# A chunked scan: masks straight from the chunk matrices' banks, two corner products with full weights

## The chip, the cores and the metric

The program runs on one core of a Trainium2 chip. The metric is the device time of one execution in microseconds; where several runs were made, their median stands. One further execution was recorded by the hardware profiler, and all rows below come from it.

## What is computed

The reference is a model of three blocks on a sequence of 1024 tokens with 1024 features, in float32: a first block with two mixers side by side (an RWKV-7 scan and an mLSTM) and a convolved feed-forward part, then two layers of gated attention. The change touches only the RWKV-7 scan, 8 heads of 64 channels:

```
def rwkv7_scan(r, w, k, v, a, b):
    def step(S, inp):
        r_t, w_t, k_t, v_t, a_t, b_t = inp
        sa = jnp.einsum('bhij,bhj->bhi', S, a_t)
        S = S * w_t[:, :, None, :] + sa[..., None] * b_t[:, :, None, :] + v_t[..., :, None] * k_t[..., None, :]
        y = jnp.einsum('bhij,bhj->bhi', S, r_t)
        return S, y
```

## The kernel before

The program is written engine by engine, each with its own list of instructions and semaphores between them. Nothing is scheduled by a tool: the order of each list is the order written.

The scan works on chunks of 64 tokens, two chunks (e = 0, 1) at a time, eight pairs in all, each for 8 heads (h, with j = h // 2 and q = h % 2). With the decays folded into `AR` (rates and receptances, features on partitions) and `BK` (keys and gains), a chunk's recurrence becomes products of 64 x 64 matrices and the inverse of one unit triangular matrix per head and chunk. For one pair the TensorE list is:

1. `chunk_matrices`: for each head and chunk the product gains x rates (L753, into banks 6 and 7) and its transpose (L759, banks 4 and 5); then `products(e)` (L768, banks 2e and 2e + 1), which gives for each head the whole 128 x 128 matrix of keys and gains against rates and receptances; then transposes of values (L775), keys (L781) and rates (L784).
2. `inverse`: it starts from the diagonal blocks (`i_X`) and joins blocks of growing size in five levels. Level n is `corner(n)` (L800: the part `i_O[n]` off the diagonal, times `i_X`), then a VectorE addition of the identity (`i_T`, L2450), then `joined(n)` (L825 and L827), whose results ScalarE (L1730, L1734) and VectorE (L2445) copy back to `i_X` and `i_XT`. After level 0's corner `flip` (L812) makes `i_XT`. Level 4 ends in `last` (L841). Each step is done in two halves of four heads, so that the copies of one half lie beside the products of the other.
3. Between these steps stand the pieces of the previous pair's `chain`: value products (L882), two halves of the solve (L899), transitions (L910), inputs (L921), the state and carried products (L931, L944) and local ones (L951). They use the solved inverse of the pair before.

VectorE masks the first product to `i_LT` (L2429), the second to `i_X` (L2433), adds the identity (L2435) and copies the values (L2437, L2438). GpSimd then makes the five `i_O[n]` from `i_LT` (L481), one operation each, and masks both copied matrices `GB` (L487). ScalarE copies `products(e)` to `GB` (L1714), the transposed keys behind them (L1719), which also frees bank 4 for the value products, and the rates (L1722). In level 1 it copies the solution (L1699, L1700) after VectorE's `W` (L2393), ahead of `i_X` for corner 2. The masks themselves (`level_masks`) are made once on GpSimd; `i_X` of the first pair waits for the last of them.

Of the kernel before, what the change touches and what calls it, by code (L numbers as in the profile page):

```python
# [20 lines left out]
ALU = mybir.AluOpType  # L21
ACT = mybir.ActivationFunctionType

P = 128
# [82 lines left out]
def build(nc, xin, vec, w_lora, consts, cmask, rope, lnm, band, ws, park, out):  # L107
    with ExitStack() as ctx:
# [105 lines left out]
        LEVELS, MASK_STEPS = 5, 18  # L214
# [29 lines left out]
        i_O = [at(f"off{n}", YH + (4 + n) * 2 * K, [P, 8, CH]) for n in range(LEVELS)]  # L244
        i_Z = at("inv_z", YH + 18 * K, [P, 8, CH])
# [165 lines left out]
        def _(pool):  # L411
# [37 lines left out]
            def level_masks():  # L449
# [21 lines left out]
                pool.wait_ge(sem("rp_done"), 4)  # L471
                merge(MSK_LOW, 7, 1)
# [4 lines left out]
            def chunk_pair(i):  # L477

                pool.wait_ge(sem("c_LT"), 2 * i + 1)
                for n in range(LEVELS):  # L480
                    pool.tensor_tensor(i_O[n][:, :, :], i_LT[:, :, :],  # L481
                                       msk[:, MSK_LEVEL[n], :].unsqueeze(1).to_broadcast([P, 8, CH]), ALU.mult
                                       ).then_inc(sem("c_off"), 1)
# [27 lines left out]
        def _(pe):  # L511
# [229 lines left out]
            def chunk_matrices(i):  # L741
# [8 lines left out]
                for h in range(8):  # L750
                    j, q = h // 2, h % 2
                    for e in range(2):
                        mm = pe.matmul(bank(6 + q)[rows(e), j * CH:(j + 1) * CH], gains(j, q, i, e), rates(j, q, c + e),  # L753
                                       start=True, stop=True)
                mm.then_inc(sem("c_Q"), 1)
                for h in range(8):
                    j, q = h // 2, h % 2
                    for e in range(2):
                        mm = pe.matmul(bank(4 + q)[rows(e), j * CH:(j + 1) * CH], rates(j, q, c + e), gains(j, q, i, e),  # L759
# [13 lines left out]
                pe.wait_ge(sem("c_LT"), 2 * i + 1)  # L773
# [4 lines left out]
                pe.wait_ge(sem("c_LT"), 2 * i + 2)  # L778
# [8 lines left out]
            def inverse(i, pieces):  # L787

                def corner(n, beside=None):  # L790
                    for half in range(2):
# [6 lines left out]
                        for h in range(4 * half, 4 * half + 4):  # L798
                            for e in range(2):
                                mm = pe.matmul(bank(inv_set(n, half))[own_rows(e), h % 4 * CH:(h % 4 + 1) * CH],  # L800
                                               i_O[n][rows(e), h, :], i_X[rows(e), h, :], start=True, stop=True)
# [4 lines left out]
                def flip():  # L806

                    pe.wait_ge(sem("c_Gcopied"), 2 * i + 2)
                    for half in range(2):
                        for h in range(4 * half, 4 * half + 4):  # L810
                            for e in range(2):
                                mm = pe.matmul(bank(inv_set(1, half))[own_rows(e), h % 4 * CH:(h % 4 + 1) * CH],  # L812
                                               i_X[rows(e), h, :], ident[rows(e), rows(e)], start=True, stop=True)
# [2357 lines left out]
```

## Time and profile before

| | us |
|---|---|
| median of 3 runs | 3541.15 (3540.38 to 3541.54) |
| the profiled execution | 3542.03 |
| its span from the first to the last instruction | 3540.2 |

```profile
PE 89%; DVE 6%; ACT 2%; issue 1%; POOL 1%; DMA 1%; ACTq 0%; DVEq 0%; POOLq 0%; SPq 0%
```

This line of the page is the chain of work that ended last, followed back from the last instruction, in shares of the span by engine. PE is TensorE's matmuls, PEld its weight loads, which overlap them, DVE is VectorE, ACT ScalarE, POOL GpSimd and SP SyncE. Matmuls are pipelined, so the length of one is more than its share of TensorE's time: what a row of them costs is read from their starts, or from the length of the whole row less the last one's own length. In the rows below x32 is the number of instructions, and what stands in brackets behind a row is the idle time ahead of it and what ended it.

### The profile page before, as it was taken

How to read it: one execution, taken by the hardware profiler on the slowest of the kernel's cores; microseconds unless marked ns; L12 is line 12 of the kernel's file. 1: busy time of each engine (PE TensorE's matmuls, PEld its weight loads, DVE VectorE, ACT ScalarE, POOL GpSimd, SP SyncE). 2: the span in 40 equal slices, each digit the busy share in tenths (PEclk: the TensorE clock that was granted, in tenths of full speed). 3: DMA queues.
4: the chain of work that ended last, by engine and by line, in shares of the span. 5: the costliest groups of instructions: out<-in, count | busy, mean ns of one | idle time of the engine just before them, and what ended most of it. 6: DMA issues, size and time to landing. Idle time of an engine off the chain costs nothing.

```text
span 3540.2 us, 55064 instructions
## 1 busy us (share of the span) xinstructions
PE 3374.2 (95%) x22562; PEld 2700.3 (76%) x22562; DVE 1872.9 (53%) x2515; ACT 781.1 (22%) x1269; POOL 1203.2 (34%) x571
## 2 busy tenths in 40 slices
PE   7999598999999999989999999999989999999997
PEld 6878488788888888867777678888867677688886
DVE  7444655546676676664545554433546554434434
ACT  4211443211101101133323320000323332300001
POOL 3324044233444443332222224434322222244444
PEclk9999699999999999999999999999999999999998
DMA  4111000221111111131112121111321111211111
GB/s 138 42 64 41 1 4 4 75 72 48 47 47 47 47 47 52 43 115 54 43 48 54 37 84 48 47 49 52 109 65 43 48 42 48 78 48 48 47 48 66
DMA packets 55226, 189.56 MB, mean 54 GB/s; under 512 B 6448, under 2 KB 15376, under 8 KB 53408
## 3 DMA queue, kind: packets, MB, share of 16 engines
q1 hardware_dynamic: 38016, 135.85, 12.1%
q10 hardware_dynamic: 17056, 51.44, 4.6%
q8 instruction: 123, 2.02, 0.2%
q14 instruction: 31, 0.25, 0.0%
HBM read 165.07 MB, written 14.86 MB: 51 GB/s over the span
## 4 chain that ended last, share of the span: by engine, by line
PE 89%; DVE 6%; ACT 2%; issue 1%; POOL 1%; DMA 1%; ACTq 0%; DVEq 0%; POOLq 0%; SPq 0%
PE ps L527 55%; PE ps L1041 10%; PE ps L1425 5%; PE ps L1213 3%; PE ps L1240 3%; PE ps L1258 3%; DVE sc L2787 1%; PE ps L800 1%; PE ps L1167 1%; PE ps L1069 1%; PE ps L825 1%; PE ps L768 1%; PE ps L899 0%; DVE hL L2287 0%; DMA cMo<-out 0%
## 5 line engine op out<-in xcount | busy, mean ns | idle before, releaser
L417 POOL TENSOR_TENSOR wH<-wraw,pv 128x1024 fp32r<-128x1024 f32 x239 | 465.1, 1946 | 2105.6 <-PE ps L527 1711.5
L527 PE MATMUL ps<-hH,wH 128*128 128x512 f32 x2800 | 880.3, 396 | 30.9 <-DVE hL L2287 11.8
L527 PE MATMUL ps<-hL,wH 128*128 128x512 f32 x2800 | 872.5, 393 | 0.0
L527 PE MATMUL ps<-hH,wL 128*128 128x512 f32 x2800 | 870.5, 392 | 0.0
L527 PEld LDWEIGHTS ps<-hH,wH 128*128 128x128 f32 x2800 | 522.0, 189 | 142.5 <-issue 20.6
L419 POOL TENSOR_TENSOR wL<-wraw,wH 128x1024 fp32r<-128x1024 f32 x239 | 623.2, 2607 | 18.8
L527 PEld LDWEIGHTS ps<-hL,wH 128*128 128x128 f32 x2800 | 525.9, 189 | 110.5 <-issue 1.7
L527 PEld LDWEIGHTS ps<-hH,wL 128*128 128x128 f32 x2800 | 525.5, 189 | 108.6
L2569 DVE TENSOR_TENSOR xT<-ps,xT 128x512 f32<-128x512 f32 x544 | 361.5, 689 | 6.6 <-PE ps L1069 6.6
L2890 DVE TENSOR_TENSOR sg<-ps,mrows 128x1024 f32<-128x1024 f32 x46 | 56.3, 1225 | 372.0 <-PE ps L527 372.0
L1928 ACT ACTIVATE sc<-sc,stat 128x256 f32<-128x256 f32 (+7 forms) x256 | 170.9, 668 | 126.9 <-DVE stat L2794 66.4
L1213 PE MATMUL ps<-kP,qP 64*128 64x256 f32 (+3 forms) x672 | 139.4, 514 | 44.3 <-DVE stat L2794 40.9
L2030 ACT ACTIVATE sg<-sg 128x1024 f32<-128x1024 f32 x46 | 48.8, 1061 | 557.9 <-DVE sg L2890 557.9
L1240 PEld LDWEIGHTS ps<-cst,sc 128*128 128x128 f32 x900 | 99.6, 144 | 77.1 <-issue 64.6
L1240 PE MATMUL ps<-cst,sc 128*128 128x128 f32 x900 | 152.7, 291 | 4.2 <-ACT sc L1928 4.1
L1213 PEld LDWEIGHTS ps<-kP,qP 64*128 64x128 f32 x672 | 56.4, 192 | 103.8 <-DVE stat L2794 47.8
L1258 PE MATMUL ps<-pt,vtok 128*64 128x128 f32 x1800 | 128.1, 282 | 0.0
L1041 PE MATMUL ps<-gH,wH 128*128 128x512 f32 x320 | 125.8, 393 | 0.0
L1041 PE MATMUL ps<-gL,wH 128*128 128x512 f32 x320 | 124.7, 390 | 0.0
L1041 PE MATMUL ps<-gH,wL 128*128 128x512 f32 x320 | 124.7, 390 | 0.0
L1258 PEld LDWEIGHTS ps<-pt,vtok 128*64 128x64 f32 x1800 | 97.4, 138 | 24.8 <-issue 23.9
L2787 DVE CUSTOM_DVE_ANT_0 sc<-ps,lnM 128x128 f32<-128x128 f32 (+7 forms) x96 | 72.7, 757 | 71.4 <-PE ps L1213 66.7
(434 smaller groups left out, 4301.7 us busy)
## 6 DMA issues: line engine op xcount, KB each, us to landing
wraw<-ws SPq DMA_DIRECT2D x242, 512.0 KB, 3.6
park<-xT ACTq DMA_DIRECT2D x2, 4096.0 KB, 13.2
xT<-park ACTq DMA_DIRECT2D x2, 4096.0 KB, 12.3
recT<-out ACTq DMA_DIRECT2D x28, 256.0 KB, 3.9
xT<-xin SPq DMA_DIRECT2D x4, 1024.0 KB, 9.1
xT<-xin ACTq DMA_DIRECT2D x1, 4096.0 KB, 12.4
sc<-kraw ACTq DMA_DIRECT2D x32, 128.0 KB, 2.4
out<-xT SPq DMA_DIRECT2D x16, 256.0 KB, 2.1
```

Source lines behind the costliest of these rows:

```text
L417: pool.tensor_tensor(wH[:, j, :], wraw[:, j, :], zero, ALU.add).then_inc(w_hi, 1)
L419: pool.tensor_tensor(wL[:, j, :], wraw[:, j, :], wH[:, j, :], ALU.subtract).then_inc(w_ready[j], 1)
L527: mm = pe.matmul(pair(p)[:, half * HALF:(half + 1) * HALF], wp, hp[:, k, half * HALF:(half + 1) * HALF], start=(m == 0 and n == 0), stop=( ...
L1041: mm = pe.matmul(pair(2 + e % 2)[:, half * HALF:(half + 1) * HALF], w[:, j, e * P:(e + 1) * P], h[:, half * HALF:(half + 1) * HALF], start ...
L1213: mm = pe.matmul(outs[j][:, c:e], qP[r, n * P:(n + 1) * P], kP[r, k0 + c - c0:k0 + e - c0], start=True, stop=True)
L1240: mm = pe.transpose(out[:, c:c + P], (SC[0] if br == "C" else SC[n % 2])[:, j, b + c:b + c + P], ident)
L1258: mm = pe.matmul(out[r, :], vtok[:, v + 64 * j:v + 64 * j + 64], pt[:, j, b + c:b + c + P], start=(c == c0), stop=(c + P == c1))
L1425: mm = pe.matmul(pair(p)[:, half * HALF:(half + 1) * HALF], wp, hp[:, k, half * HALF:(half + 1) * HALF], start=(k == k0 and n == 0), stop= ...
L1928: act.activation(buf[:, j, b + c0:b + c1], buf[:, j, b + c0:b + c1], ACT.Exp, bias=stat[:, S_NEG, s:s + 1], accum_out=stat[:, S_DEN, s:s + ...
L2569: ins = dve.tensor_tensor(x, bank(2 * pairs[e % len(pairs)] + half), x, ALU.add)
L2787: dve.tensor_tensor_reduce(buf[:, j, b + c0:b + c1], bank(0, 4)[:, o + c0:o + c1], bias, 1.0, -3e38, op, ALU.max, mx).then_inc(sem("at_ttr ...
L2890: dve.tensor_tensor(gates[g], pair(j), mrows[:, :], ALU.mult).then_inc(sem("sg_raw"), 1)
```

## The change

In each pair the product gains x rates (L753) is dropped. The same block is a quarter of what `products(e)` computes, on the partitions 64 to 127 for chunk 0 and 0 to 63 for chunk 1, and VectorE masks it from there into `i_LT`, one operation for each chunk on 64 partitions. So `i_LT` and all that follows from it in the inverse lie on the opposite halves from before, and the slices of partitions change places in `corner`, `flip`, `joined` and `last`. `c_LT` now counts three steps per pair (i_X, then i_LT of chunk 0 and of chunk 1); GpSimd starts after the third, and ScalarE's copy of each matrix waits until VectorE has read it. The corners 1 and 2 get weights of 128 x 128 per head (`i_F`), in which the two chunks' blocks stand off the diagonal and the rest is zero, through two masks of twice the width (`f_msk`), which GpSimd makes in eight more steps; each is then one product per head over the whole array, where there were two in quarters.

```
--- before.py
+++ after.py
@@ -211,7 +211,7 @@
         MSK_LOW, MSK_EYE = 0, 7
-        LEVELS, MASK_STEPS = 5, 18
+        LEVELS, MASK_STEPS = 5, 26
         INV_ACT, INV_DVE, INV_PROD = 12, 18, 30
         MSK_LEVEL = (2, 3, 6, 5, 4)
         eye = msk[:, MSK_EYE, :]
@@ -242,6 +242,9 @@
         AT = [at(f"AT{n}", YH + (5 + n) * TILE, [P, 8, 2 * CH]) for n in range(2)]
         i_LT, i_X, i_XT, i_T = [at(f"inv{n}", YH + n * 2 * K, [P, 8, CH]) for n in range(4)]
         i_O = [at(f"off{n}", YH + (4 + n) * 2 * K, [P, 8, CH]) for n in range(LEVELS)]
+        FULL = (1, 2)
+        i_F = {n: at(f"full{n}", o, [P, 8, 2 * CH]) for n, o in zip(FULL, (YH + 10 * K, YH + 28 * K))}
+        f_msk = at("full_msk", XA + 28 * K, [P, len(FULL), 2, CH])
         i_Z = at("inv_z", YH + 18 * K, [P, 8, CH])
         W = at("W", WR + 4 * TILE, [P, 8, CH])
         MT = at("MT", YL + TILE, [P, 2, 4, CH])
@@ -469,6 +472,11 @@
                 step(pool.tensor_tensor(m(3), m(3), m(2), ALU.subtract))
                 step(pool.tensor_tensor(m(2), m(2), m(1), ALU.subtract))
                 pool.wait_ge(sem("rp_done"), 4)
+                for k, n in enumerate(FULL):
+                    for e in range(2):
+                        home, away = (slice(64, 128), slice(0, 64)) if e == 0 else (slice(0, 64), slice(64, 128))
+                        step(pool.memset(f_msk[away, k, e, :], 0.0))
+                        step(pool.tensor_copy(f_msk[home, k, e, :], msk[home, MSK_LEVEL[n], :]))
                 merge(MSK_LOW, 7, 1)
                 step(pool.tensor_tensor(m(MSK_LOW), m(MSK_LOW), m(7), ALU.subtract))
                 step(pool.tensor_tensor(m(MSK_LOW), m(MSK_LOW), m(1), ALU.subtract))
@@ -476,8 +484,15 @@
             def chunk_pair(i):
-                pool.wait_ge(sem("c_LT"), 2 * i + 1)
+                pool.wait_ge(sem("c_LT"), 3 * i + 3)
                 for n in range(LEVELS):
+                    if n in FULL:
+                        shape = [P, 8, 2, CH]
+                        pool.tensor_tensor(i_F[n][:, :, :].rearrange("p h (e t) -> p h e t", e=2),
+                                           i_LT[:, :, :].unsqueeze(2).to_broadcast(shape),
+                                           f_msk[:, FULL.index(n), :, :].unsqueeze(1).to_broadcast(shape), ALU.mult
+                                           ).then_inc(sem("c_off"), 1)
+                        continue
                     pool.tensor_tensor(i_O[n][:, :, :], i_LT[:, :, :],
                                        msk[:, MSK_LEVEL[n], :].unsqueeze(1).to_broadcast([P, 8, CH]), ALU.mult
                                        ).then_inc(sem("c_off"), 1)
@@ -750,13 +765,7 @@
                 for h in range(8):
                     j, q = h // 2, h % 2
                     for e in range(2):
-                        mm = pe.matmul(bank(6 + q)[rows(e), j * CH:(j + 1) * CH], gains(j, q, i, e), rates(j, q, c + e),
-                                       start=True, stop=True)
-                mm.then_inc(sem("c_Q"), 1)
-                for h in range(8):
-                    j, q = h // 2, h % 2
-                    for e in range(2):
-                        mm = pe.matmul(bank(4 + q)[rows(e), j * CH:(j + 1) * CH], rates(j, q, c + e), gains(j, q, i, e),
+                        mm = pe.matmul(bank(4 + q)[own_rows(e), j * CH:(j + 1) * CH], rates(j, q, c + e), gains(j, q, i, e),
                                        start=True, stop=True)
                 mm.then_inc(sem("c_Q"), 1)
@@ -770,12 +779,11 @@
                     mm.then_inc(sem("c_G"), 1)
                 products(0)
-                pe.wait_ge(sem("c_LT"), 2 * i + 1)
                 for j in range(4):
                     mm = pe.transpose(bank(7)[:, j * P:(j + 1) * P], vpad[:, j, (c + 1) * CH:(c + 3) * CH], ident)
                 mm.then_inc(sem("c_tokT"), 1)
                 products(1)
-                pe.wait_ge(sem("c_LT"), 2 * i + 2)
+                pe.wait_ge(sem("c_LT"), 3 * i + 1)
                 for e in range(2):
                     for j in range(4):
                         mm = pe.transpose(bank(4 + e)[:, j * P:(j + 1) * P], BK[:, j, i, e * P:(e + 1) * P], ident)
@@ -796,9 +804,14 @@
                         else:
                             pe.wait_ge(sem("inv_act"), i * INV_ACT + 3 * n - 2 + half)
                         for h in range(4 * half, 4 * half + 4):
+                            at_h = slice(h % 4 * CH, (h % 4 + 1) * CH)
+                            if n in FULL:
+                                mm = pe.matmul(bank(inv_set(n, half))[:, at_h], i_F[n][:, h, :], i_X[:, h, :],
+                                               start=True, stop=True)
+                                continue
                             for e in range(2):
-                                mm = pe.matmul(bank(inv_set(n, half))[own_rows(e), h % 4 * CH:(h % 4 + 1) * CH],
-                                               i_O[n][rows(e), h, :], i_X[rows(e), h, :], start=True, stop=True)
+                                mm = pe.matmul(bank(inv_set(n, half))[rows(e), at_h], i_O[n][own_rows(e), h, :],
+                                               i_X[own_rows(e), h, :], start=True, stop=True)
                                 if beside:
                                     beside(h, e)
                         mm.then_inc(sem("inv_prod"), 1)
@@ -809,8 +822,8 @@
                     for half in range(2):
                         for h in range(4 * half, 4 * half + 4):
                             for e in range(2):
-                                mm = pe.matmul(bank(inv_set(1, half))[own_rows(e), h % 4 * CH:(h % 4 + 1) * CH],
-                                               i_X[rows(e), h, :], ident[rows(e), rows(e)], start=True, stop=True)
+                                mm = pe.matmul(bank(inv_set(1, half))[rows(e), h % 4 * CH:(h % 4 + 1) * CH],
+                                               i_X[own_rows(e), h, :], ident[own_rows(e), own_rows(e)], start=True, stop=True)
                         mm.then_inc(sem("inv_prod"), 1)
                 def joined(n):
@@ -822,10 +835,10 @@
                         for h in range(4 * half, 4 * half + 4):
                             for e in range(2):
                                 at_h = slice(h % 4 * CH, (h % 4 + 1) * CH)
-                                x = pe.matmul(bank(inv_set(n + 1, half))[rows(e), at_h], i_XT[own_rows(e), h, :],
-                                              i_T[own_rows(e), h, :], start=True, stop=True)
-                                xt = pe.matmul(bank(inv_set(n, half))[own_rows(e), at_h], i_T[own_rows(e), h, :],
-                                               i_XT[own_rows(e), h, :], start=True, stop=True)
+                                x = pe.matmul(bank(inv_set(n + 1, half))[own_rows(e), at_h], i_XT[rows(e), h, :],
+                                              i_T[rows(e), h, :], start=True, stop=True)
+                                xt = pe.matmul(bank(inv_set(n, half))[rows(e), at_h], i_T[rows(e), h, :],
+                                               i_XT[rows(e), h, :], start=True, stop=True)
                         x.then_inc(sem("inv_prod"), 1)
                         xt.then_inc(sem("inv_prod"), 1)
@@ -839,7 +852,7 @@
                         for h in range(4 * half, 4 * half + 4):
                             for e in range(2):
                                 mm = pe.matmul(bank(inv_set(n + 1, half))[rows(e), h % 4 * CH:(h % 4 + 1) * CH],
-                                               i_T[own_rows(e), h, :], i_XT[own_rows(e), h, :], start=True, stop=True)
+                                               i_T[rows(e), h, :], i_XT[rows(e), h, :], start=True, stop=True)
                         mm.then_inc(sem("inv_prod"), 1)
                 corner(0, pieces and pieces["values"])
@@ -1711,6 +1724,7 @@
                 p = i % 2
                 for e in range(2):
                     act.wait_ge(sem("c_G"), i * 2 + e + 1)
+                    act.wait_ge(sem("c_LT"), 3 * i + e + 2)
                     act.activation(GB[p][:, e, :, 0:2 * CH].rearrange("p (j q) x -> p q j x", q=2),
                                    bank(2 * e, 2).rearrange("p (q j x) -> p q j x", q=2, x=P), ACT.Copy
                                    ).then_inc(sem("c_Gcopied"), 1)
@@ -2425,13 +2439,17 @@
                 def mask4(n):
                     return n.unsqueeze(1).unsqueeze(1).to_broadcast([P, 2, 4, CH])
-                dve.wait_ge(sem("c_Q"), 2 * i + 1)
-                dve.tensor_tensor(by_parity(i_LT), stacked(6), mask4(cst[:, C_G, 0:CH]), ALU.mult).then_inc(sem("c_LT"), 1)
-                dve.wait_ge(sem("c_Q"), 2 * i + 2)
+                dve.wait_ge(sem("c_Q"), i + 1)
                 if i == 0:
                     dve.wait_ge(sem("pool_own"), MASK_STEPS + 1)
                 dve.tensor_tensor(by_parity(i_X), stacked(4), mask4(msk[:, MSK_LOW, :]), ALU.mult).then_inc(sem("c_LT"), 1)
-                dve.wait_ge(sem("c_LT"), 2 * i + 2)
+                for e in range(2):
+                    home = slice(64, 128) if e == 0 else slice(0, 64)
+                    dve.wait_ge(sem("c_G"), 2 * i + e + 1)
+                    block = ps[home, 2 * e:2 * e + 2, :].rearrange("p q (j x) -> p q j x", x=P)[:, :, :, 0:CH]
+                    upper = cst[home, C_G, 0:CH].unsqueeze(1).unsqueeze(1).to_broadcast([64, 2, 4, CH])
+                    dve.tensor_tensor(by_parity(i_LT)[home], block, upper, ALU.mult).then_inc(sem("c_LT"), 1)
+                dve.wait_ge(sem("c_LT"), 3 * i + 1)
                 dve.tensor_tensor(i_X[:, :, :], i_X[:, :, :], mask(eye, 8), ALU.add).then_inc(sem("c_X"), 1)
                 dve.wait_ge(sem("c_tokT"), 4 * i + 1)
                 dve.tensor_copy(UV[i % 2][0:64, 0, :, :], bank(7)[0:64, :])
```

## Rows read from the trace of the kernel before

**Rows 1.** The page: busy time of each engine, its share of the span.

```profile
PE 3374.2 (95%) x22562; PEld 2700.3 (76%) x22562; DVE 1872.9 (53%) x2515; ACT 781.1 (22%) x1269; POOL 1203.2 (34%) x571
```

**Rows 2.** Windows, a chunk pair and the scan: PE, PEld, DVE, ACT, POOL, clock, DMA.

```profile
510.80:536.80 26.00, 23.56 (x821) 21.29 (x819) 13.67 (x29) 9.82 (x21) 11.29 (x7) 1.00 0.02 4
...
438.50:642.30 203.80, 184.04 (x6273) 166.45 (x6274) 107.06 (x217) 76.55 (x164) 91.16 (x59) 0.99 0.02 4
```

**Rows 3.** Waits of TensorE in the scan: total us, times, longest.

```profile
PE ps L827 <- issue: 3.5, 4, 1.2
...
PE ps L800 <- ACT inv L1730: 1.9, 4, 0.5
...
PE ps L910 <- issue: 0.2, 1, 0.2
```

**Rows 4.** Windows from idle time to idle time, weight loads alone (PEld busy, count).

```profile
584.98:588.62 3.64, 2.44 (x126) 1.00 0.02 5
588.62:592.60 3.98, 3.53 (x127) 1.00 0.03 6
```

**Rows 5.** DMA queues in the scan's stretch.

```profile
q8 instruction: 49, 0.80, 1.7%
```

**Rows 6.** Timeline of the start of a pair: start us, length us, what, count.

```profile
512.10 0.64 PE L759 MATMUL ps<-BK,AR 64*64 64x64 f32 x30
512.33 0.69 DVE L2429 TENSOR_TENSOR inv<-ps,cst 128x512 f32<-128x512 f32 x1 [0.82 <-PE ps L753]
...
513.65 1.27 DVE L2435 TENSOR_TENSOR inv<-inv,msk 128x512 f32<-128x512 f32 x1
...
514.85 0.67 DVE L2437 COPY UV<-ps 64x512 f32<-64x512 f32 x1
515.44 1.09 PE L781 MATMUL ps<-cst,BK 128*128 128x128 f32 x8
...
515.56 1.02 ACT L1714 ACTIVATE GB<-ps 128x1024 f32<-128x1024 f32 x1 [0.65 <-PE ps L768]
516.37 0.60 PE L784 MATMUL ps<-cst,AR 128*128 128x128 f32 x4
516.48 1.08 ACT L1719 ACTIVATE GB<-ps 128x512 f32<-128x512 f32 x2
516.90 0.32 PE L800 MATMUL ps<-inv,off 64*64 64x64 f32 x2
517.12 0.27 PE L882 MATMUL ps<-UV,GB 64*64 64x64 f32 x1
```

**Rows 7.** Timeline of GpSimd: the last masks, and one pair.

```profile
438.58 0.29 POOL L458 TENSOR_TENSOR msk<-msk 128x64 f32<-128x64 f32 x1 [85.44 <-DVE BK L2385]
...
439.35 0.32 POOL L474 TENSOR_TENSOR msk<-msk 128x64 f32<-128x64 f32 x1
...
513.10 6.66 POOL L481 TENSOR_TENSOR off<-inv,msk 128x512 f32<-128x512 f32 x5 [15.62 <-DVE inv L2429]
519.69 4.69 POOL L487 TENSOR_TENSOR GB<-GB,cst 128x1024 f32<-128x1024 f32 x2
```

**Rows 8.** Timelines from corner 1 to corner 2: TensorE, VectorE and ScalarE.

```profile
521.80 1.13 PE L800 MATMUL ps<-inv,off 64*64 64x64 f32 x32
522.50 0.89 DVE L2450 TENSOR_TENSOR inv<-ps,msk 128x256 f32<-128x256 f32 x2 [1.31 <-PE ps L800]
523.31 0.68 DVE L2393 COPY W<-ps 128x512 f32<-128x512 f32 x1
...
524.62 0.59 ACT L1700 ACTIVATE UV<-ps 64x512 f32<-64x512 f32 x1
525.12 0.64 ACT L1730 ACTIVATE inv<-ps 128x256 f32<-128x256 f32 x2
...
525.63 1.15 PE L800 MATMUL ps<-inv,off 64*64 64x64 f32 x32
```

**Rows 9.** Timeline of TensorE: full weights with one moving column.

```profile
1543.64 1.93 PE L540 MATMUL ps<-cst,nsum_g 128*128 128x1 f32 x16
```

More of the change, by code:

```diff
@@ L244, in build @@
         i_O = [at(f"off{n}", YH + (4 + n) * 2 * K, [P, 8, CH]) for n in range(LEVELS)]
+        FULL = (1, 2)
+        i_F = {n: at(f"full{n}", o, [P, 8, 2 * CH]) for n, o in zip(FULL, (YH + 10 * K, YH + 28 * K))}
+        f_msk = at("full_msk", XA + 28 * K, [P, len(FULL), 2, CH])
         i_Z = at("inv_z", YH + 18 * K, [P, 8, CH])
@@ L471, in level_masks @@
                 pool.wait_ge(sem("rp_done"), 4)
+                for k, n in enumerate(FULL):
+                    for e in range(2):
+                        home, away = (slice(64, 128), slice(0, 64)) if e == 0 else (slice(0, 64), slice(64, 128))
+                        step(pool.memset(f_msk[away, k, e, :], 0.0))
+                        step(pool.tensor_copy(f_msk[home, k, e, :], msk[home, MSK_LEVEL[n], :]))
                 merge(MSK_LOW, 7, 1)
@@ L477, in chunk_pair @@
             def chunk_pair(i):
[L479 removed]
+                pool.wait_ge(sem("c_LT"), 3 * i + 3)
                 for n in range(LEVELS):
+                    if n in FULL:
+                        shape = [P, 8, 2, CH]
+                        pool.tensor_tensor(i_F[n][:, :, :].rearrange("p h (e t) -> p h e t", e=2),
+                                           i_LT[:, :, :].unsqueeze(2).to_broadcast(shape),
+                                           f_msk[:, FULL.index(n), :, :].unsqueeze(1).to_broadcast(shape), ALU.mult
+                                           ).then_inc(sem("c_off"), 1)
+                        continue
                     pool.tensor_tensor(i_O[n][:, :, :], i_LT[:, :, :],
@@ L752, in chunk_matrices @@
                     for e in range(2):
[L753 to L759, printed above, removed]
+                        mm = pe.matmul(bank(4 + q)[own_rows(e), j * CH:(j + 1) * CH], rates(j, q, c + e), gains(j, q, i, e),
                                        start=True, stop=True)
@@ L798, in corner @@
                         for h in range(4 * half, 4 * half + 4):
+                            at_h = slice(h % 4 * CH, (h % 4 + 1) * CH)
+                            if n in FULL:
+                                mm = pe.matmul(bank(inv_set(n, half))[:, at_h], i_F[n][:, h, :], i_X[:, h, :],
+                                               start=True, stop=True)
+                                continue
                             for e in range(2):
-                                mm = pe.matmul(bank(inv_set(n, half))[own_rows(e), h % 4 * CH:(h % 4 + 1) * CH],
-                                               i_O[n][rows(e), h, :], i_X[rows(e), h, :], start=True, stop=True)
+                                mm = pe.matmul(bank(inv_set(n, half))[rows(e), at_h], i_O[n][own_rows(e), h, :],
+                                               i_X[own_rows(e), h, :], start=True, stop=True)
                                 if beside:
@@ L811, in flip @@
                             for e in range(2):
-                                mm = pe.matmul(bank(inv_set(1, half))[own_rows(e), h % 4 * CH:(h % 4 + 1) * CH],
-                                               i_X[rows(e), h, :], ident[rows(e), rows(e)], start=True, stop=True)
+                                mm = pe.matmul(bank(inv_set(1, half))[rows(e), h % 4 * CH:(h % 4 + 1) * CH],
+                                               i_X[own_rows(e), h, :], ident[own_rows(e), own_rows(e)], start=True, stop=True)
                         mm.then_inc(sem("inv_prod"), 1)
```

28 lines of the change are left out of this document (16 added, 12 removed).

## The prediction

> **What bounds the kernel now.** I began with the page's line of busy times [rows 1]: TensorE is busy for 95% of the span. The profiled execution took 3542.03 us against a median of 3541.15, so a change of the profile's length can be added to the median as it stands. A stretch that grows on TensorE's queue moves the end by as much, if nothing there was waiting. The change touches only the scan, which the stretches by chunk pair place between 438.5 and 642.3 us, with a period of some 26 us [rows 2]. There TensorE's busy column reads 184.0 of 203.8 us, but that doesn't say that the array is at its peak, so the second question was what ends its idle times. The list of waits has ten rows "issue" for TensorE in the scan, 3.5 us the longest and 0.2 the shortest; their sum is 16.6 us in 26 idle times, and the only other steady row is 1.9 us behind ScalarE's copy [rows 3]. "Issue" means that nothing in the profile was waited for. What it is can be read by laying windows from the end of one such idle time to the end of the next: each holds 126 or 127 weight loads and as many matmuls, some 253 instructions with the waits between them left out, and takes 3.64 or 3.98 us [rows 4]. The scan's weight loads and matmuls together (6273 and 6274) divided by 256 are 49, and the queue for instructions moved 49 packets of 16 KB in it [rows 2, 5]. So TensorE's instructions arrive in blocks of 256, a block can't be entered before about 3.75 us have gone since the last one was entered, and dense stretches of small products run ahead of that. The scan has two limits that alternate: this delivery of instructions, and the chain product, VectorE or ScalarE copy, next product.
>
> The Trainium skill, Runtime: NRT & Kernel Launch, section "Instruction fetch mechanics", gives the same 16 KB and 256 instructions, but says that the fetch is hidden behind the issue of the instructions. The 26 idle times speak against that here; if it held, the give-back below would be nothing and the time 3561.6.
>
> **The change part by part**, per chunk pair, of which there are eight.
>
> *Removed: the 16 products of L753.* Each is two passes (32 records per pair). Their twin L759 uses all four quarters of the array too: 30 passes in 0.64 us, of which 0.22 is the last one's own length, so 15 ns a pass [rows 6]. 32 x 15 ns is **0.49 us** less, all on TensorE's queue.
>
> *The start of the inversion.* Before, VectorE masks i_LT (0.69 us) and i_X as well, and adds the identity (1.27) while TensorE still makes the chunk matrices [rows 6]. Afterwards i_LT comes out of the banks of these matrices, in two halves of 64 partitions. A copy of 64 x 512 takes 0.67 us where one of 128 x 512 takes 0.69 [rows 6], so halving the partitions saves nothing: two operations of 0.68, the second only after the last matrix. Behind that second one wait: ScalarE's copy of the second matrix (it now waits for c_LT too; 1.02 us) with the copies of the keys queued behind it (a pair in 1.08 us), which free bank 4 for the value products; GpSimd's first off-diagonal mask (five in 6.66 us, 1.3 each [rows 7]); and, queued on VectorE itself, the addition of the identity. Today the copy starts at 515.56 and the first value product at 517.12, 1.56 later [rows 6]. Now 0.69 goes in front of it: 2.25 after the last matrix. The mask gives 0.69 + 1.3 and two handovers of some 0.05, 2.1; the identity 0.69 + 1.27 and one handover, 2.0. All three arrive together, so the cost is 0.7 to 0.8; I take **0.75**. The values' copies (c_X) then end near 518.5 in these times, and VectorE's first eye addition slips by about a microsecond, but the first solve product (16 passes in about 0.9 us) lies between it and the joined product, so this stays covered. If that cover were gone it would cost up to 0.5.
>
> *Two corners with full weights.* Corner 1 is 32 passes of 64 by 64 from 521.80, 1.13 us with the last one's 0.22: 28 ns a pass, or 57 per pair of quarters [rows 8]. Now it is 8 products, 16 passes, with 128 x 128 weights and 64 columns moving. No row of before has this form. The nearest are the 16 passes with 128 x 128 weights and a single moving column: 1.93 us less 0.25 over 15 intervals, 112 ns [rows 9]; and the transposes with 128 columns moving: 8 in 1.09 less 0.28 over 7, 116 [rows 6]. One column or 128 cost the same, so here it is the loading of 128 weight columns that counts, and 64 moving columns lie between the two. The other end is 57 ns, if a full load went as fast as the two quarters that it replaces. I take 112, since both neighbours stand on either side of the new shape: 16 x 0.112 = 1.79 against 0.91, **0.88** more per corner, 1.76 for the two. Is it on the path? After corner 1 VectorE makes T (0.89 for both halves), then copies W (0.68), ScalarE copies UV twice (0.59 each) and i_X (0.64 for two), and only then corner 2 starts [rows 8]. The whole corner is in front of that chain. Behind corner 2 TensorE's own queue goes on with products that wait for nothing late. So both count in full.
>
> *Going between tile sizes.* From the last 128 x 128 transpose to the first 64 x 64 product TensorE takes longer than within either: the four transposes begin at 516.37 and step by some 0.11, so the last begins at 516.70, and the product comes at 516.90, 0.20 later [rows 6]. In minus the steady step I take 0.10 for leaving full size and 0.15 for entering it (there also the second pass comes late), so **0.50** per pair; the ends are 0, where a wait covers it, and 0.7. The Trainium skill, TensorEngine Tiling (Array Packing), section "Tiling Modes", says that a change of mode drains the engine, which speaks against putting two full corners amid quarters. The trace agrees, by the 0.20. Without such a cost the time forecast would be 3550.6.
>
> *Masks and GpSimd.* The masks FULL for corners 1 and 2 have 1024 elements per partition rather than 512; the nearest row is 4.69 for two, 2.35 each, against 1.3 [rows 7]: GpSimd works 2.1 us more per pair and starts 3 us later. Corner 1's mask is then ready at about 519.9 and starts to be wanted at 521.80, corner 2's at 522.3 against 525.6; the masked GB at 530 is wanted by the next pair after 540. Nothing. Once only, eight more small steps stand before X's mask: three take from 438.58 to 439.67 [rows 7], so 3 us more, mostly under the first pair's matrices: 0.3 in all.
>
> *Instructions.* L753's 32 passes and the 16 saved in each full corner are 64 passes, 128 instructions with their loads, of some 1640 per pair; 1024 over the scan, four blocks. If every block were waited for, this returned 4 x 3.75 = 15 us. Of 49 blocks 26 are, so I take half, **7 us** in total; the ends are 0 and 15.
>
> **Sum:** 8 x (-0.49 + 0.75 + 1.76 + 0.50) + 0.3 = 20.5; less 7 is +13.5. On the profiled execution 3555.5, on the median **3554.6**.
>
> **The rivals.**
> *A, the other side: delivery of instructions is the real bound.* If a block costs 3.75 us whatever is in it, the added array time falls into idle time that is there anyway, and 128 instructions fewer give 1.9 us per pair, 15 in all: 3526. For it: a block's mean time in the scan is 203.8/49 = 4.16 us, close to 3.75. Against: the idle time for it is 16.6 us in all, and lies in the second half of each pair, while corners 1 and 2 and the start lie in the first, where blocks take five and more. It decides from where the added 20.5 us falls by more than two thirds into those idle times. With cheap full loads (57 ns) the same mechanism gives 20.5 - 14 - 4 - 7, 3536.6. Chance 0.13.
> *B, about even:* half of the added time is covered by blocks that were late anyway, and the return is 12: 8 x 2.5 x 0.7 - 12 = +2, 3543. Chance 0.15.
> *C, nothing comes back:* blocks stay as late as they are, since the dense second half hardly changes; +20.5 and dearer changes of tile size 1.6: 3563. For it: in that half only L753 goes. Chance 0.12, within the slower cases.
> That the change doesn't do what it says isn't a rival: the products and their quarters are plain in the diff.
>
> **How the numbers follow.** The forecast and C together have 0.72, A 0.13, B 0.15. About 0.2% (7 us) is what a measurement of this kernel can tell from no change: slower by more 0.72, within it 0.15, faster 0.13. The range leaves out A and reaches over most of B and up to C: 3541 to 3563.
>
> **What would show it.** In the profile after: L753's pass over the gains gone; L800 in two forms, the full one with 256 records, 16 to a corner in about 2.0 us from first to last end (right: 105 to 120 ns a pass; 60 or 80 would take the forecast away); the value products 2.2 to 2.4 us behind the last matrix; the scan some 13.5 us longer; four packets of instructions fewer and the "issue" rows near 10 us rather than 16.6. If these rows fall to nearly nothing, A or B was right; if they stay at 16, C.

## The result and the profile after

The changed kernel takes 3549.23 us at the median of 13 runs, the one before 3541.15. The ratio is 1.0024, with a 95% interval of 1.0015 to 1.0033: slower by 8.5 us, between 5.3 and 11.7. So it lies between 3546.5 and 3552.9. The forecast was 3554.6 within 3541 to 3563: the range holds the measured time, but the forecast itself lies above the interval.

The profiled executions differ by a little more, 3553.22 against 3542.03 us; the first is the second slowest of its 13 runs. All scans below are from one execution each. First the stretch of the scan in both, from its first product to the first product behind it (columns: length, then busy time and count for PE, PEld, DVE, ACT and POOL, the granted clock, the share of the DMA engines, GB/s). Before:

```profile
438.50:654.00 215.50, 193.37 (x6528) 174.84 (x6528) 111.17 (x225) 78.92 (x168) 91.16 (x59) 0.99 0.02 4
```

After:

```profile
438.90:665.60 226.70, 201.64 (x6017) 182.66 (x6017) 111.52 (x233) 78.92 (x168) 109.32 (x67) 0.99 0.02 4
```

The scan is 11.2 us longer; the rest of the span is the same within half a microsecond. TensorE is busy for 8.3 us more with 511 matmuls fewer, and idle for 25.1 instead of 22.1. What it is idle for (waits of TensorE in the scan: total us, times, longest) has changed:

```profile
PE ps L813 <- POOL off L496: 8.4, 8, 1.1
PE ps L809 <- ACT inv L1744: 3.4, 7, 0.5
PE ps L944 <- issue: 2.9, 4, 1.1
PE ps L813 <- issue: 1.7, 2, 0.9
PE ps L957 <- issue: 1.6, 2, 0.9
PE ps L840 <- issue: 1.5, 3, 0.7
PE ps L964 <- issue: 1.3, 2, 0.7
PE ps L838 <- issue: 0.8, 2, 0.6
```

The "issue" rows, which answer to those of [rows 3], sum to 9.8 us in 15 idle times, where it was 16.6 in 25 (the prediction counts 26, but the ten rows sum to 25). A new wait stands above them: in each of the eight pairs corner 0 (now L813) waits for GpSimd's first mask. It can be followed in the timeline of one pair, which answers to [rows 6]:

```profile
519.55 1.09 PE L789 MATMUL ps<-cst,BK 128*128 128x128 f32 x8
519.67 0.68 DVE L2451 TENSOR_TENSOR inv<-ps,cst 64x512 f32<-64x512 f32 x1 [0.99 <-PE ps L777]
520.28 0.67 DVE L2453 TENSOR_TENSOR inv<-inv,msk 128x512 f32<-128x512 f32 x1
520.43 1.65 POOL L496 TENSOR_TENSOR off<-inv,msk 128x512 f32<-128x512 f32 x1 [14.05 <-DVE inv L2451]
520.45 1.02 ACT L1728 ACTIVATE GB<-ps 128x1024 f32<-128x1024 f32 x1 [0.64 <-DVE inv L2451]
520.48 0.60 PE L792 MATMUL ps<-cst,AR 128*128 128x128 f32 x4
...
521.37 1.08 ACT L1733 ACTIVATE GB<-ps 128x512 f32<-128x512 f32 x2
...
522.13 0.27 PE L813 MATMUL ps<-inv,off 64*64 64x64 f32 x1 [1.05 <-POOL off L496]
522.24 0.24 PE L895 MATMUL ps<-UV,GB 64*64 64x64 f32 x1
```

The second chunk matrix is there at 519.67, and the first value product (L895) comes at 522.24, 2.57 us later, where it was 1.56 (515.56 to 517.12 in [rows 6]). GpSimd's mask takes 1.65 us, and TensorE begins right behind it. The full corners in the same pair, which answer to [rows 8]:

```profile
527.03 2.00 PE L809 MATMUL ps<-inv,full 128*128 128x64 f32 x16
530.15 1.10 PE L923 MATMUL ps<-GB,W 64*64 64x128 f32 x32
531.73 1.97 PE L809 MATMUL ps<-inv,full 128*128 128x64 f32 x16 [0.48 <-ACT inv L1744]
533.63 0.69 PE L934 MATMUL ps<-UV,GB 128*64 128x64 f32 x16
```

Sixteen passes take 2.00 us. Less the last one's 0.27 over 15 intervals that is 115 ns a pass: 160 ns for the first interval and 111 or 112 for all others. From the last of them to the first product in quarters it takes 0.2 us. In the DMA view the queue for instructions moved 48 packets where the same stretch of before had 52.

### The profile page after: what moved, and what is told of

It reads as the page before. It is cut to its first block, busy times and chain, and to the rows that moved or that the text cites. A ratio compares the mean times of both kernels' runs of the same rounds, so it can differ in the third digit from the quotient of the medians.

```text
span 3550.9 us, 54071 instructions
## 1 busy us (share of the span) xinstructions
PE 3381.5 (95%) x22050; PEld 2706.4 (76%) x22050; DVE 1874.0 (53%) x2523; ACT 781.6 (22%) x1269; POOL 1222.6 (34%) x579
## 4 chain that ended last, share of the span: by engine, by line
PE 89%; DVE 6%; ACT 2%; issue 1%; POOL 1%; DMA 1%; ACTq 0%; DVEq 0%; POOLq 0%; SPq 0%
PE ps L542 55%; PE ps L1054 10%; PE ps L1438 5%; PE ps L1226 3%; PE ps L1253 3%; PE ps L1271 3%; DVE sc L2805 1%; PE ps L809 1%; PE ps L1180 1%; PE ps L1082 1%; PE ps L813 1%; PE ps L777 1%; PE ps L838 1%; PE ps L912 0%; POOL off L496 0%
```

## Experiments

The theory that the first of them test: the change's time is array time (the full loads) and a later start, less part of what the delivery of instructions takes (by the prediction's reading a block of 256 can't be entered before some 3.75 us have passed since the last). The rival is A of the prediction: the delivery decides, and array time in the scan is nearly free. Since the time outside the scan differs between the profiled executions, from 3316.7 to 3324.7 us without the two padded ones, each result stands with its ratio to the kernel before and with its scan in the profile.

**1. No full corners.** The changed kernel, with all corners in quarters.

```diff
-        FULL = (1, 2)
+        FULL = ()
```

> The changed kernel with all five corners in quarters again; only the separate product is dropped and masked from the chunk matrices. My theory (array time and chain): per pair the product saves 0.49 us and the start of the inversion waits 0.75 to 1.05, so +2.1 to +4.5 us in eight pairs; 64 instructions fewer per pair, two blocks in all, give back half of 7.5: together -1.7 to +0.7 us against the kernel before, 3539.5 to 3541.9. Rival A (delivery of instructions is the bound): -7.5 us, 3533.6. By my theory the issue rows of TensorE in the scan sum to some 13 us and the wait for GpSimd's first mask to some 8 us.

Ratio 1.0015 (1.0006 to 1.0025), so +5.3 us.

```profile
441.80:664.20 222.40, 190.90 (x6273) 171.17 (x6273) 111.73 (x233) 78.83 (x168) 90.46 (x59) 0.99 0.02 4
```

The line of corner 0 is L812 here:

```profile
PE ps L812 <- POOL off L495: 8.4, 8, 1.1
```

Outside both expectations: the half of the change that I had at nothing costs 6.9 us of scan, more than the whole rest. TensorE is busy for 2.5 us less (8 x 0.49 had been 3.9), but idle for 9.4 more; 8.4 of these are the wait for GpSimd's mask, and the issue rows sum to 17.7 us, not less than before's 16.6. For the instructions that were dropped nothing came back.

**2. Full corners only.** The kernel before, its products kept, with `i_F` and `f_msk` as in the changed one.

```diff
+                            if n in FULL:
+                                mm = pe.matmul(bank(inv_set(n, half))[:, h % 4 * CH:(h % 4 + 1) * CH], i_F[n][:, h, :],
+                                               i_X[:, h, :], start=True, stop=True)
+                                continue
```

> The kernel before with only the full weights in corners 1 and 2; the separate product stays. My theory: 16 passes of 112 ns for 0.91 us per corner, and 0.25 for entering and leaving, 2.26 us per pair, 18.1 in all, less half of two blocks (3.75): +14.3 us, 3555.5. If the parts add up to the 8.1 us measured for both and the first experiment is near nothing, this one is at +7 to +10 instead, and then the full corners' price is what I had too high. Rival A: -7.5 us or at most 0, since the array time would fall into idle time. Rival: cheap full loads, -3.75 us.

Ratio 1.0011 (1.0002 to 1.002), +3.9 us (0.7 to 7.1). The +14.3 of my theory is excluded.

```profile
438.70:657.30 218.60, 204.67 (x6272) 186.97 (x6272) 112.14 (x226) 78.88 (x168) 110.06 (x67) 0.99 0.02 4
```

TensorE is busy for 11.3 us more, but idle for only 13.9 instead of 22.1 us; the issue rows sum to 7.4. So the array time is paid, and more than two thirds of it (8.2 us) come back as less idle time: the waits for instructions fall by 9.2 us, and the one for ScalarE's copy rises from 1.9 to 3.4. The scan of experiment 1 and of this one stand 6.9 and 3.1 us over before's, together 10.0 of the 11.2.

**3. Corner 1 alone in full.**

```diff
-        FULL = (1, 2)
+        FULL = (1,)
```

> The changed kernel with only corner 1 in full weights, corner 2 in quarters. My theory: each full corner costs the same, since both are in front of a chain on TensorE's queue, so this lies halfway between the changed kernel and the one without full corners: about +4 us against the kernel before. If corner 1 alone is expensive (its whole length is ahead of the chain through W, UV and i_X) and corner 2 is covered, it lies at the changed kernel's +8 us; if corner 1 is covered, at the first experiment's time.

Ratio 1.0016 (1.0007 to 1.0025), +5.7 us; a scan of 222.8 us, busy 196.3. That is the first experiment's time, not halfway to the changed kernel, though the intervals would allow either; the issue rows fell from 17.7 to 11.5 us. The busy time is 5.4 us over the first experiment's and 5.3 under the changed kernel's: in array time the two corners cost the same. That corner 1 would be covered by something of its own isn't shown.

**4. The values' transposes later.** Experiment 1's kernel, one step moved.

```diff
                 products(0)
+                products(1)
                 for j in range(4):
                     mm = pe.transpose(bank(7)[:, j * P:(j + 1) * P], vpad[:, j, (c + 1) * CH:(c + 3) * CH], ident)
                 mm.then_inc(sem("c_tokT"), 1)
-                products(1)
```

> The first experiment's kernel, with the transposes of the values moved from between the two chunk matrices to behind the second. The second matrix then is done 0.59 us earlier while TensorE's work ahead of corner 0 is the same. If the start of the inversion is limited by the chain matrix, VectorE, GpSimd/ScalarE, as I say, the wait for GpSimd's mask falls from about 1.05 us per pair to about 0.5 and the time by 3 to 4.5 us against the first experiment (3536 to 3538). If delivery of instructions is the bound (rival A), it is the same as the first experiment within 1 us.

Ratio 0.9996 (0.9987 to 1.0005), 1.4 us under the kernel before and 6.7 under experiment 1; the scan is 215.6 us long.

```profile
441.30:656.90 215.60, 188.20 (x6272) 171.06 (x6272) 111.71 (x233) 78.08 (x168) 90.51 (x59) 0.99 0.02 4
PE ps L812 <- POOL off L495: 4.9, 8, 0.6
```

The wait went down from 8.4 to 4.9 us, as expected, and the scan by 6.8. So the wait is on the path: when the matrix is there earlier, TensorE starts earlier. But the scan fell by nearly twice the wait, and the rest is something else. TensorE is busy for 2.7 us less, and in the list by line this lies with the neighbours of the step that was moved: the chunk matrices (64 x 128) fell from 20.2 to 18.5 us, the transposes of the values (128 x 128) from 5.7 to 5.2, those of the keys (128 x 128) from 8.7 to 8.3. TensorE now goes from the one tile size to the other once in this stretch and not three times, which would explain it but wasn't tried by itself. The issue rows fell by 1.2 us more (17.7 to 16.5). The saving in busy time would be open to the kernel before as well; its own version with late values wasn't run, so that this kernel is 1.4 us under it doesn't say that the dropped product pays.

**5. An earlier start.** On top of that, ScalarE copies chunk 0's keys ahead of the second matrix, and GpSimd makes the first mask in two halves.

```diff
+                    if n == 0:
+                        for g in (slice(0, 4), slice(4, 8)):
+                            pool.tensor_tensor(i_O[n][:, g, :], i_LT[:, g, :],
+                                               msk[:, MSK_LEVEL[n], :].unsqueeze(1).to_broadcast([P, 4, CH]), ALU.mult
+                                               ).then_inc(sem("c_off"), 1)
+                        continue
```

> The kernel without full corners and with late values, plus two changes of order at the start of the inversion: ScalarE copies the keys of chunk 0 (which frees bank 4) ahead of the second matrix, and GpSimd makes the first off-diagonal mask in two halves of four heads, so that corner 0 can begin on the first. My theory: the wait for GpSimd's mask (4.9 us in the scan, 0.6 per pair) falls to nearly nothing, 0.3 to 0.5 us per pair: -2.5 to -4 us against the one with late values only, some 3534. If delivery of instructions takes back what is saved (as I suspect for time saved in dense stretches), no change; but this time is saved in a stretch of slow blocks, so I expect it to stay.

Ratio 0.9988 (0.9979 to 0.9996), 4.2 us faster than the kernel before (1.4 to 7.4), with a median of 3534.86 us. This is the one kernel that clearly beats both; how much of that is the late values alone isn't shown. One of its twelve runs took 14612.5 us; it isn't in the ratio, and its cause is open.

```profile
441.20:653.80 212.60, 188.39 (x6273) 170.93 (x6273) 111.71 (x233) 78.10 (x168) 91.66 (x67) 0.99 0.02 4
```

The wait for GpSimd is gone from the list and the scan is 3.0 us shorter than in 4, where the wait had been 4.9.

**6 and 7. The same products twice, in two places.** The kernel before, `joined` of level 0 or of level 3 issued twice.

```diff
-                        for h in range(4 * half, 4 * half + 4):
+                        for h in [h for _ in range(2 if n == 3 else 1) for h in range(4 * half, 4 * half + 4)]:
```

> The kernel before with the products of joined, level 0, issued twice (same result): 64 more passes in quarters, 0.93 us of array time and 128 instructions per pair, in the first half of a pair where blocks of 256 instructions take five us and more. Both theories: +0.93 us per pair, 7.4 us, if array time alone counts. My theory of delivery: the blocks here have time to spare, so about +7 to +8 us, and the issue rows stay near their 16.6 us.

> The same doubling in level 3, the second half of a pair, where blocks are waited for: the same 0.93 us of array time and 128 instructions. If only array time and the chain count: +7.4 us as in the other. My theory of delivery: half a block more per pair that costs 3.75 us whatever is in it, 1.9 us per pair, up to +15 us; the issue rows grow by some 7 us. The difference between the two kernels is the test.

Ratios 1.0033 (1.002 to 1.0046) and 1.0038 (1.0025 to 1.0051), and two scans of 229.4 us, 13.9 over before's in either place.

```profile
438.40:667.80 229.40, 201.87 (x7040) 182.50 (x7040) 110.89 (x225) 78.87 (x168) 91.20 (x59) 0.99 0.02 4
```

My theory that the place decides fell: both cost the same. But the doubled products make TensorE busy for only 8.5 us more (8 x 0.93 had been 7.4), and idle for 5.4 more; the issue rows rise to 21.5 and 19.7 us. 1024 instructions are four blocks; 13.9 / 4 is 3.5 us a block, near the 3.75 read from the distances of the edges. In these two kernels added dense products cost more than their array time, and about what their instructions cost by that reading.

**8. The changed kernel with late values.** The step of experiment 4, in the changed kernel.

```diff
                 products(0)
+                products(1)
                 for j in range(4):
                     mm = pe.transpose(bank(7)[:, j * P:(j + 1) * P], vpad[:, j, (c + 1) * CH:(c + 3) * CH], ident)
                 mm.then_inc(sem("c_tokT"), 1)
-                products(1)
```

> The changed kernel (full corners 1 and 2) with the values' transposes behind the second chunk matrix. If parts add up: the full corners cost the 3 to 4 us by which the changed kernel stands over the one without them, and the later values save 5 to 7, so +1 to +3 us against the kernel before, and 3 to 4 above the one with late values and quarter corners. If full corners pay once the start is not waited for, it is at or below that one.

Ratio 1.0017 (1.0008 to 1.0025), +6.0 us; a scan of 226.2 us, half a microsecond under the changed kernel's. The wait for the mask fell from 8.4 to 5.0 us as in 4, but here the issue rows rose from 9.8 to 14.4. What was saved at the start came back as waiting for instructions. So in the scans the parts don't add up: full corners cost 3.1 us on the kernel before, and 10.6 on top of experiment 4. The runs point the same way, 3.9 us (0.7 to 7.1) against some 7, but too widely to show it.

**9. Corners with twice the columns.** The kernel before; in corners 1 and 2 each product moves its 64 columns twice, and only the first copy is used.

```diff
+                                x_h = i_X[rows(e), h:h + 1, :].to_broadcast([CH, 2, CH]) if wide else i_X[rows(e), h, :]
```

> The kernel before with corners 1 and 2 in quarters as they were, but each product moves its 64 columns twice (128 columns, the second copy unused). A pair of quarters should then take about 110 ns, as long as a full product takes, at the old number of instructions. So it has the array time of the full corners and twice their instructions, 64 more per pair than the kernel with full corners only. If array time and chain alone count: the same as that kernel, scan +3 us. If the delivery of instructions counts (3.5 us per 256, as the two doubled kernels gave): 7 us more, scan +10 us against before.

Ratio 1.0024 (1.0014 to 1.0033), +8.5 us, but a scan only 4.3 us over before's.

```profile
438.30:658.10 219.80, 203.59 (x6528) 185.31 (x6528) 110.74 (x225) 78.92 (x168) 91.10 (x59) 0.99 0.02 4
```

TensorE is busy for 10.2 us more, nearly as with full corners (11.3), at the old number of instructions, and idle for 5.9 less. So it is mainly the array time that takes the place of the waiting, not the instructions saved: these make 1.2 us of scan between this kernel and experiment 2's, where I had expected 7, and 1.2 is too little to be read from two scans (experiments 10 and 11). By the ratios the two differ by 4.6 us, by their medians over those of the kernel before (6.8 and 5.2) by 1.6; the intervals overlap (1.0014 to 1.0033 and 1.0002 to 1.002), so the runs don't tell the two apart.

**10 and 11. Padding ahead of the scan.** 32 products of no use, in TensorE's wait before the scan, on the kernel before and on the changed one.

```diff
+            for _ in range(32):
+                pe.matmul(bank(7)[:, 0:2], cst[:, C_BLK, :], cst[:, C_BLK, 0:P:64], start=True, stop=True)
             pe.wait_ge(sem("rp_done"), 4)
```

> The kernel before with 32 small products (128 instructions with their loads) that are of no use, in the 11 us in which TensorE waits ahead of the scan. They cost no time there, but move the edges of the blocks of 256 by half a block against the scan's steps. If what is measured between kernels hangs on where the edges fall, this moves the scan by some us, either way; if only the number of blocks counts, by less than 1.5 us.

> The same padding ahead of the changed kernel's scan. If the change's +11 us of scan hangs on where the edges of the blocks fall, it changes by several us; if it is array time, chain and number of blocks, the scan stays within 1.5 us of 226.6 us.

```profile
430.42 13.82 PE L1113 MATMUL ps<-cst 128*128 128x2 f32 x64
```

The padding wasn't free: its passes took 216 ns, not 112, since the granted clock reads 0.50 in this stretch (1.2 GHz), so it outlasted the wait and the scan began at 444.2 and 443.1. The whole times (ratios 1.0016 and 1.0025) hold that too and say little. The scans are 216.6 and 224.5 us long, +1.1 and -2.2 against the same kernels without padding; some 0.4 of the 1.1 is the first pair, whose corner 0 comes 7.8 us after the scan's start and not 7.4. So where the edges of the blocks fall moves a scan by up to 2 us, and a difference between two scans by more: with the padding in both kernels the change makes 7.9 us of scan and not 11.2. Nearly a third of the 11.2 may be placement, the sign and the larger part are not. A difference of scans below some 3 us isn't read in any of these experiments, and the 3.1 of experiment 2 and the 3.0 between 4 and 5 stand at that limit.

**12. The dropped product twice.** The kernel before, L753's loop run over the heads twice.

```diff
-                for h in range(8):
+                for h in [*range(8), *range(8)]:
```

> The kernel before with the product gains x rates (the one that the change drops) issued twice: 0.49 us of array time and 64 instructions per pair more. Array time alone: +3.9 us. Delivery at 3.5 us per 256 instructions: +7 us. If doubling costs 7 and dropping it gave nothing, then dropping must have cost as much somewhere else, in the wait at the start of the inversion.

Ratio 1.0017 (1.0008 to 1.0026), +6.0 us (2.8 to 9.2), and a scan of 221.5, also +6.0.

```profile
439.70:661.20 221.50, 197.78 (x6785) 179.05 (x6785) 111.01 (x225) 78.83 (x168) 91.17 (x59) 0.99 0.02 4
```

The interval holds both expectations, 3.9 and 7, and the scan lies between them. TensorE is busy for 4.4 us more and idle for 1.6, and the issue rows hardly rose (16.9 against 16.6). So most of it is array time here, unlike in experiments 6 and 7; that the cost follows the instructions isn't shown for this product. Nor is it symmetrical: issued twice it adds 4.4 us of busy time, dropped it took away 2.5.

## Why the prediction was right, and where it was not

The sign and the range hold: +13.5 was forecast, +11.2 is in the profile and +8.5 (5.3 to 11.7) in the runs. Three of its rows hold as well: the full product's price, a wait at the start of the inversion, and issue rows that fall to about 10 us. But that the total came so near is in part luck: the two halves of the change, run singly, both fell far from what these terms give, on opposite sides. So the terms have to be gone through singly.

*The full product's price was right.* 112 ns a pass had been taken from rows with one and with 128 moving columns [rows 9, 6]; measured are 111 to 112 with 64. The cheap end (57 ns) is gone.

*Full corners as a whole were sized too high.* I had 2.26 us per pair. Measured from the first pass of a corner to the next step: corner 1 takes 1.93 us (527.03 to the joined products at 528.96 in the timeline after) against 1.18 before, corner 2 1.90 against 1.08, together 1.57 more. The way into corner 1, from the last pass before it, takes 0.20 against 0.08; into corner 2 TensorE waits for ScalarE either way. That makes 1.69. The 0.50 for changes of tile size was the failed step: corner 2 had changed its tile before too (to L921's), and behind corner 1 TensorE had waited for VectorE. T's first half, the first of the two operations in [rows 8], ends at 522.92, and the joined products came at 522.98, about 0.2 later than the corner's passes alone would have let them; the longer corner covers that. In eight pairs 2.26 for 1.69 is 4.6 us too much. The prices themselves were right, 0.20 us from the last pass to the first on the way in and on the way out. What failed was to count them as new time. The rule of the Trainium skill, TensorEngine Tiling (Array Packing), section "Tiling Modes", that a change of mode drains the engine, isn't contradicted: the 0.2 us on the way out agree.

*The start of the inversion was sized too low.* The three things that I said would arrive together are there, but GpSimd's first mask takes 1.65 us and not 1.3. It was to be had from the trace before: the five masks in 6.66 us of [rows 7] are four of 1.27 to 1.29 and one of 1.72. Another pair before tells what slows one, since there VectorE's copies come apart from its addition:

```profile
538.39 1.27 POOL L481 TENSOR_TENSOR off<-inv,msk 128x512 f32<-128x512 f32 x1 [14.01 <-DVE inv L2429]
538.95 1.26 DVE L2435 TENSOR_TENSOR inv<-inv,msk 128x512 f32<-128x512 f32 x1
539.62 1.72 POOL L481 TENSOR_TENSOR off<-inv,msk 128x512 f32<-128x512 f32 x1
541.31 1.27 POOL L481 TENSOR_TENSOR off<-inv,msk 128x512 f32<-128x512 f32 x1
541.38 0.69 DVE L2438 COPY UV<-ps 64x512 f32<-64x512 f32 x1
```

The mask that has a copy beside it keeps its 1.27 us. The addition of the identity, which starts while a mask runs, takes 1.26 us where after the change it takes 0.67, and the mask behind it takes 1.72. After the change the addition comes first and the first mask, the one that TensorE waits for, is the slow one. So the delay is 1.01 per pair, not 0.75; and the wait that follows, 8.4 us in all, is the largest row of TensorE's idle time in the scan after the change.

*The return of instructions was right in total and wrong in its place.* I had 7 us; the issue rows went down from 16.6 to 9.8, 6.8 us. But I had reckoned it by instructions, which gives each half of the change the same. Experiments 1 and 2 show that the full corners brought all of it (7.4 us left), and the dropped products none (17.7). Time added to TensorE's queue between edges that are late anyway is taken out of the wait for them; experiment 9 shows it with the number of instructions unchanged. And with the dropped product, time and instructions taken away left the wait standing. That is rival A's mechanism: it is real, at two thirds of the corners' array time, but for the start of the inversion it doesn't work.

So the parts came out as +3.9 us for the full corners (3.1 of scan), where the prediction's terms give 8 x 2.26 - 3.5 = 14.6, and as +5.3 for the dropped product (6.9 of scan), where they give 8 x (-0.49 + 0.75) - 3.5 = -1.4. The sum of the two was nearer than either. The full corners' terms fail by the changes of tile size (4.6 us) and by a return of 9.2 us in the issue rows, not 3.5. The dropped product's fail by the return, where the issue rows rose by 1.1 instead of falling by 3.5; by the wait (8.4 us, not 6.0); and by the busy time saved (2.5, not 3.9).

*Smaller points.* The eight steps on GpSimd took 2.0 us, not 3, and TensorE didn't wait for them. The number of packets fell by four, as said. The masks for the full corners (2.36 us each, 522.04 after the first) were never waited for. Rival B's time of 3543 is excluded by the interval, C's 3563 too. B's text says half and its sum 0.7, which is 30% covered; with half it would have been 3539.

*What stays open:* why dropping instructions returned so little, when adding some cost 3.5 us per 256 in experiments 6 and 7 and 3.0 in 12, and why late values saved 6.8 us of scan without full corners and half a microsecond with them. Placement of the edges explains some 3 us of it.

## What to carry to other kernels

Where TensorE idles with nothing to wait for, count its instructions between such idle times: if the count is constant, the engine waits for its own program, and array time saved in such a stretch may come back as that wait. Before a product is dropped because another holds it already, look at when the other is ready: here the copy came out of a bank that is full at the end of the stage instead of at its beginning, and that cost twice what the product had. A cost in a pipeline of this kind is best measured for each part alone, since two parts that are wrong by 7 and 11 us can add up to a total that looks right.

## What the runs showed of the hardware

- TensorE's idle times in dense stretches lay one block of 256 instructions apart, 3.64 and 3.98 us in [rows 4], and the queue for instructions moved 49 packets for 49 blocks. Doubling dense products cost 3.5 us per 256 instructions, 13.9 us for 8.5 and 7.9 of busy time (experiments 6 and 7).
- A float32 pass with 128 weight columns takes 112 to 116 ns at the full clock whether 1, 64 or 128 columns move, 216 ns at half the granted clock (experiment 10); a pair of quarters with 64 takes 57.
- GpSimd's multiplication of 128 x 512 elements took 1.27 to 1.29 us alone, beside VectorE's copies out of PSUM, and when its addition of two operands in SBUF started later; it took 1.65 to 1.72 when that addition was under way or came in between; the addition took 0.67 us when it came first and 1.26 or 1.27 when the multiplication did.
- Halving the partitions of a VectorE operation saves nothing: 64 x 512 out of PSUM took 0.68 us, 128 x 512 took 0.69.
